# A hybrid layer on one core: 32x32 blocks in the triangular inverse, head sums in two fp32r passes, and another order on VectorE

## What is computed

```python
xn = rms_norm(h, norm_mix[l])
proj = xn @ w_l
y_a = chunk_band_attention(a_q, a_k, a_v, a_rel_bias[l])
y_b, v_l = rwkv7_time_mix(b_r, b_k, b_v, b_w, b_a, b_g, vmix, ...)
y_c = sliding_sink_attention(c_q, c_k, c_v, c_sinks[l], t5_bias)
h = h + concatenate([y_a, y_b, y_c]) @ w_out[l]
h = h + cross attention of rms_norm(h) into rms_norm(mem)
h = h + square(relu(rms_norm(h) @ mlp_w1[l])) @ mlp_w2[l]
return rms_norm(h, norm_final)

# in rwkv7_time_mix, per head of 64 features:
kk = kk / maximum(sqrt(sum(kk * kk)), 1e-12)           # a sum over a head's features
y = wkv7_scan(r, decay, k, v, -kk, kk * a)             # state = state*w + (state a) b + v k
var = mean(square(y - mean(y)))                        # a second one
bonus = sum(rh * kh * r_k) * vh                        # a third one
```

## Time and profile before

| what | us |
|---|---|
| median of three runs (2647.16 to 2648.95) | 2648.77 |
| the profiled execution | 2651.39 |
| its span | 2649.7 |
| TensorE busy | 2592.2 (98%) |
| VectorE busy | 1711.9 (65%) |
| ScalarE busy | 925.0 (35%) |
| GpSimd busy | 133.0 (5%) |

### The profile page before, as it was taken

The page is one execution under the profiler, slowest core; times in us unless marked ns, Lnnn a source line. Parts: engine busy times, 40 slices in busy tenths (PEclk is TensorE's granted clock), DMA queues, the critical chain, the costliest instruction groups (busy, mean ns, idle before and its releaser), DMA issues.

```text
span 2649.7 us, 45475 instructions
## 1 busy us (share of the span) xinstructions
PE 2592.2 (98%) x17994; PEld 2066.4 (78%) x17994; DVE 1711.9 (65%) x2535; ACT 925.0 (35%) x1475; POOL 133.0 (5%) x239
## 2 busy tenths in 40 slices
PE   9999999999999999998999999999999999999997
PEld 7877777777768765786878888888878888888886
DVE  6256666666634755344567677777777777777775
ACT  5222222222223644343533333333233332333324
POOL 5000101111112110000000000000000000000000
PEclk9999999999999999999999999999999999999999
DMA  4321111111125542221332332323323233232322
GB/s 168 119 62 51 50 45 50 49 50 50 49 90 202 180 133 66 88 88 48 111 105 88 112 105 95 114 87 110 111 90 113 88 110 109 91 119 87 105 88 104
DMA packets 72468, 250.13 MB, mean 94 GB/s; under 512 B 8960, under 2 KB 9088, under 8 KB 71104
## 3 DMA queue, kind: packets, MB, share of 16 engines
q1 hardware_dynamic: 65232, 222.62, 25.7%
q0 software_dynamic: 7024, 24.56, 2.9%
HBM read 236.93 MB, written 10.22 MB: 93 GB/s over the span
## 4 chain that ended last, share of the span: by engine, by line
PE 84%; DVE 8%; issue 4%; ACT 3%; DVEq 1%; DMA 0%; ACTq 0%; SPq 0%
PE ps L1435 25%; PE ps L1437 23%; PE ps L1436 23%; PE ps L1453 9%; DVE sum_lo L1334 2%; DVE b_raw L1279 1%; DVE w_lo L881 1%; DVE sums L1283 1%; PE ps L1662 1%; PE ps L1639 1%; DVE b_lo L1275 1%; ACT sums L807 1%; PE ps L1649 1%; PE ps L1447 1%; ACT b_hi L543 1%
## 5 line engine op out<-in xcount | busy, mean ns | idle before, releaser
L1435 PE MATMUL ps<-act_hi,w_hi 128*128 128x512 f32 x1792 | 730.4, 408 | 12.9 <-DVE w_lo L881 12.9
L881 DVE TENSOR_TENSOR w_lo<-w_raw,w_hi 128x1024 fp32r<-128x1024 f32 (+2 forms) x319 | 356.0, 1120 | 561.1 <-ACT w_hi L543 561.1
L1437 PE MATMUL ps<-act_hi,w_lo 128*128 128x512 f32 x1792 | 700.5, 391 | 0.0
L1436 PE MATMUL ps<-act_lo,w_hi 128*128 128x512 f32 x1792 | 700.3, 391 | 0.0
L543 ACT ACTIVATE w_hi<-w_raw 128x1024 fp32r<-128x1024 f32 (+2 forms) x319 | 310.3, 974 | 1014.6 <-PE ps L1437 1006.4
L1435 PEld LDWEIGHTS ps<-act_hi,w_hi 128*128 128x128 f32 x1792 | 336.4, 188 | 110.6 <-DVE w_lo L881 19.4
L1437 PEld LDWEIGHTS ps<-act_hi,w_lo 128*128 128x128 f32 x1792 | 336.9, 188 | 72.6
L1436 PEld LDWEIGHTS ps<-act_lo,w_hi 128*128 128x128 f32 x1792 | 337.1, 188 | 66.6 <-issue 4.3
L1435 PE MATMUL ps<-b_hi,sum_hi 128*128 128x512 f32 x848 | 330.5, 390 | 1.9 <-DVE sum_lo L1334 1.9
L1436 PE MATMUL ps<-b_lo,sum_hi 128*128 128x512 f32 x848 | 330.5, 390 | 0.0
L543 ACT ACTIVATE b_hi<-b_raw 128x1024 fp32r<-128x1024 f32 x210 | 221.1, 1060 | 302.1 <-PE ps L1437 300.4
(11 more groups left out here) (320 smaller groups left out, 2849.4 us busy)
## 6 DMA issues: line engine op xcount, KB each, us to landing
w_raw<-in_w_rest SPq DMA_DIRECT2D x200, 512.0 KB, 3.5
b_raw<-in_w_down SPq DMA_DIRECT2D x120, 512.0 KB, 3.4
w_raw<-in_w_pairs SPq DMA_DIRECT2D x112, 384.0 KB, 3.0
x_t<-in_x_turned SPq DMA_DIRECT2D x8, 512.0 KB, 8.1
qk<-scr_qkv POOLq DMA_DIRECT2D x16, 256.0 KB, 3.1
h<-in_x POOLq DMA_DIRECT2D x4, 1024.0 KB, 8.4
out<-h SPq DMA_DIRECT2D x4, 1024.0 KB, 3.9
scr_qkv<-pad POOLq DMA_DIRECT2D x15, 256.0 KB, 4.2
```

The costliest lines, as they stand in the source:

```text
L881: V.tensor_tensor(dst, w_raw[:, slot, 0:dst.shape[-1]], high.bitcast(F32), ALU.subtract).then_inc(s["w_split"], 1)
L1435: mm(dst, a_hi, b_hi, start=start, stop=False, skip_group_check=again)
L1436: mm(dst, a_hi, b_lo, start=False, stop=False, skip_group_check=again)
L1437: return mm(dst, a_lo, b_hi, start=False, stop=stop, skip_group_check=again)
```

## The change

It has four parts.

**The inverse by blocks.** LEVELS loses 32, so the levels build only the inverses of the four 32x32 diagonal blocks of a chunk (two heads x two halves). These are kept packed, four groups of 32 partitions by 8 chunks x 32 columns, 256 columns in all. The turned copy isn't kept: after each `level_t` TensorE turns `inv` (`inv_turned`), ScalarE copies it to `inv_b`, and `level_x` multiplies that by `t_level`. At the end `corner_t` and `corner_x` make the off-diagonal 32x32 corner. Each of these five is a loop of 32x32 matmuls, 32 in a call (16 for a corner). The gram for `m_ab` becomes `diagonal_grams`, 32 matmuls that read 64 rows each and write 32x32. T_PER_PAIR, X_PER_PAIR and V_PER_PAIR are the counts of semaphore steps in a pair.

**The head sums.** `ones2` and `mean2` are fp32r, and a sum is two fp32r matmuls, of the high and of the low part (`sums_of_split`). ScalarE therefore squares twice at p = 2 and p = 3 (the first one rounded to fp32r), VectorE forms the r*k product twice at p = 6, and VectorE has a new subtraction for each sum: at p = 3, at p = 4 (finishing pair), and at the end of p = 6. TensorE waits for these.

**The seam behind g = 14.** VectorE splits the first `rest` unit before the first of the three evacuations, ScalarE's high part waits for 119 used units, and the memory tokens' DMA is issued at the start of g = 13 and handled at positions 9 to 16.

**The feed-forward order.** On VectorE `up_lo(c, 2)` moves ahead of four of the `sum_low` calls and a weight sum, `up_lo(c, 3)` moves behind `op_lo` of product 3.

Tensors are also laid out anew in SBUF, and GpSimd's constants follow (fewer level masks, in more and smaller copies).

```diff
-LEVELS = [2, 4, 8, 16, 32]
+LEVELS = [2, 4, 8, 16]
...
+        def block_rows(k):
+            return slice(k * B, (k + 1) * B)
+
+        def block_cols(c, k):
+            return slice(c * L + k % 2 * B, c * L + (k % 2 + 1) * B)
+
+        def packed(c):
+            return slice(c * B, (c + 1) * B)
 
         def chunks(buf):
...
+                    nc.scalar.activation(sq_hi[:, :], kk_[:, :], ACT.Square, scale=col(prm, K_K))
...
+                    nc.scalar.activation(y2_hi[:, :], yc[:, :], ACT.Square)
...
+                if p in (14, 16, 18, 20) and elem:
+                    lv = (p - 14) // 2
+                    act.wait_ge(s["xT_mm"], V_PER_PAIR * q + lv + 1)
+                    copy(inv_b[:, :], ps[:, 5, NC * B:]).then_inc(s["xT_ev"], 1)
...
-            hi(0, UNITS * G_IN // RAW + 1, rest_slot(w_hi, 0), UNITS * G_IN)
+            hi(0, UNITS * G_IN // RAW + 1, rest_slot(w_hi, 0), UNITS * G_IN - 1)
...
+                    dve.wait_ge(s["sq_k"], q + 1)
+                    V.tensor_tensor(sq_lo[:, :], T1, sq_hi[:, :].bitcast(F32), ALU.subtract).then_inc(s["sq_split"], 1)
+                if p == 4 and fin:
+                    dve.wait_ge(s["ysq_ready"], f + 1)
+                    V.tensor_tensor(y2_lo[:, :], ysq[:, :], y2_hi[:, :].bitcast(F32),
+                                    ALU.subtract).then_inc(s["var_split"], 1)
...
-                    V.scalar_tensor_tensor(T1, rr[:, :], rk_col, kp[:, :], ALU.mult, ALU.mult).then_inc(s["bon_in"], 1)
+                    V.scalar_tensor_tensor(sq_hi[:, :], rr[:, :], rk_col, kp[:, :], ALU.mult, ALU.mult)
+                    V.scalar_tensor_tensor(T1, rr[:, :], rk_col, kp[:, :], ALU.mult, ALU.mult)
...
+                    V.tensor_tensor(sq_lo[:, :], T1, sq_hi[:, :].bitcast(F32), ALU.subtract).then_inc(s["bon_in"], 1)
...
-                    dve.wait_ge(s["mab_mm"], q + 1)
-                    masked(m_ab, 4, mk_lo[:, :])
...
+                    V.tensor_tensor(packed_chunks(inv[:, :]), packed_chunks(ps[:, 4, 0:NC * B]), over_chunks(mk_1[:, :]),
+                                    ALU.mult)
...
-                    dve.wait_ge(s["t_mm"], LV * q + lv + 1)
-                    masked(t_lev, 4, mk_lev[:, lv, :]).then_inc(s["t_ev"], 1)
+                    dve.wait_ge(s["t_mm"], T_PER_PAIR * q + lv + 1)
+                    if lv < len(LEVELS):
+                        V.tensor_tensor(packed_chunks(t_lev[:, :]), packed_chunks(ps[:, 4, 0:NC * B]),
+                                        over_chunks(mk_lev[:, lv, :]), ALU.mult).then_inc(s["t_ev"], 1)
+                    else:
+                        V.tensor_copy(t_lev[:, :], ps[:, 4, 0:NC * B]).then_inc(s["t_ev"], 1)
+                        dve.wait_ge(s["xT_mm"], V_PER_PAIR * q + lv + 1)
+                        masked(invT[par], 3, mk_upi[:, :]).then_inc(s["xT_ev"], 1)
...
+                    if lv < len(LEVELS):
+                        dve.wait_ge(s["x_mm"], X_PER_PAIR * q + lv + 1)
+                        V.tensor_tensor(inv[:, :], inv[:, :], ps[:, 5, 0:NC * B], ALU.add).then_inc(s["x_ev"], 1)
...
+                        if g == G_IN - 1 and u == UNITS - 1 and third == 0:
+                            lo(UNITS * G_IN, 0, rest_slot(w_lo, 0), rest_slot(w_hi, 0))
                         if g and u == UNITS - 1:
                             evacuate(g, third)
 
-            lo(UNITS * G_IN, 0, rest_slot(w_lo, 0), rest_slot(w_hi, 0))
...
                 sum_low(c - 1, A12, 2, 4)
+                up_lo(c, 2)
                 sum_low(c - 1, S2, 4, 4)
...
                         op_lo(c - 1, n + 2)
+                        if n == 1:
+                            up_lo(c, 3)
                         if n == 5:
...
+            def diagonal_grams(b, lhsT, rhs):
+                for c in range(NC):
+                    for k in (0, 2, 1, 3):
+                        hf, cols = HALF[k // 2], block_cols(c, k)
+                        last = mm(ps[block_rows(k), b, packed(c)], lhsT[hf, cols], rhs[hf, cols], start=True, stop=True)
...
+            def level_t(b):
+                for c in range(NC):
+                    for k in range(4):
+                        rows = block_rows(k)
+                        last = mm(ps[rows, b, packed(c)], m_abT[rows, block_cols(c, k)], inv[rows, packed(c)],
+                                  start=True, stop=True)
...
+            def level_x(b):
+                for c in range(NC):
+                    for k in range(4):
+                        rows = block_rows(k)
+                        last = mm(ps[rows, b, packed(c)], inv_b[rows, packed(c)], t_lev[rows, packed(c)],
+                                  start=True, stop=True)
...
+            def inv_turned(dst):
+                for c in range(NC):
+                    for k in range(4):
+                        rows = block_rows(k)
+                        last = mm(dst(c, k), inv[rows, packed(c)], eye_b[rows, :], start=True, stop=True)
...
+            def corner_t(b):
+                for c in range(NC):
+                    for k in (0, 2):
+                        last = mm(ps[block_rows(k + 1), b, packed(c)], m_abT[block_rows(k), block_cols(c, k + 1)],
+                                  inv[block_rows(k), packed(c)], start=True, stop=True)
...
+            def corner_x(b, whole):
+                for c in range(NC):
+                    for k in (0, 2):
+                        rows, cols = block_rows(k + 1), block_cols(c, k + 1)
+                        last = mm(ps[block_rows(k), b, cols], t_lev[rows, packed(c)], whole[rows, cols],
+                                  start=True, stop=True)
...
+            def sums_of_split(b, weights, high, low):
+                mm(bank(b), weights[:, :], high[:, :], start=True, stop=False)
+                return mm(bank(b), weights[:, :], low[:, :], start=False, stop=True)
...
                 if p == 4 and elem:
-                    pe.wait_ge(s["sq_k"], q + 1)
+                    pe.wait_ge(s["sq_split"], q + 1)
                     pe.wait_ge(s["zw_ev"], q + 1)
-                    mm(bank(4), ones2[:, :], T1, start=True, stop=True).then_inc(s["ss_mm"], 1)
+                    sums_of_split(4, ones2, sq_hi, sq_lo).then_inc(s["ss_mm"], 1)
...
-                    pe.wait_ge(s["ysq_ready"], f + 1)
+                    pe.wait_ge(s["var_split"], f + 1)
...
-                    mm(bank(3), mean2[:, :], ysq[:, :], start=True, stop=True).then_inc(s["var_mm"], 1)
...
+                    sums_of_split(3, mean2, y2_hi, y2_lo).then_inc(s["var_mm"], 1)
...
-                    mm(bank(5), ones2[:, :], T1, start=True, stop=True).then_inc(s["bon_mm"], 1)
+                    sums_of_split(5, ones2, sq_hi, sq_lo).then_inc(s["bon_mm"], 1)
...
-                    grams(4, aT[par], aa).then_inc(s["mab_mm"], 1)
+                    diagonal_grams(4, aT[par], aa)
...
                         grams(3, aa, rT[par]).then_inc(s["mrb_mm"], 1)
                         pe.wait_ge(s["inv_init"], q + 1)
                     else:
-                        pe.wait_ge(s["x_ev"], (LV - 1) * q + lv)
-                    grams(4, m_abT, inv).then_inc(s["t_mm"], 1)
+                        pe.wait_ge(s["x_ev"], X_PER_PAIR * q + lv)
+                    if lv < len(LEVELS):
+                        level_t(4).then_inc(s["t_mm"], 1)
+                        inv_turned(lambda c, k: ps[block_rows(k), 5, NC * B + c * B:NC * B + (c + 1) * B]
+                                   ).then_inc(s["xT_mm"], 1)
+                    else:
+                        corner_t(4).then_inc(s["t_mm"], 1)
+                        pe.wait_ge(s["mrb_ev"], q + 1)
+                        inv_turned(lambda c, k: ps[block_rows(k), 3, block_cols(c, k)]).then_inc(s["xT_mm"], 1)
...
-                    pe.wait_ge(s["t_ev"], LV * q + lv + 1)
-                    if lv:
-                        pe.wait_ge(s["xT_ev"], LV * q + lv)
-                    if lv < LV - 1:
-                        grams(5, invT[par], t_lev).then_inc(s["x_mm"], 1)
-                    pe.wait_ge(s["mrb_ev"], q + 1)
-                    grams(3, t_lev, invT[par]).then_inc(s["xT_mm"], 1)
+                    pe.wait_ge(s["t_ev"], T_PER_PAIR * q + lv + 1)
+                    pe.wait_ge(s["xT_ev"], V_PER_PAIR * q + lv + 1)
+                    if lv < len(LEVELS):
+                        level_x(5).then_inc(s["x_mm"], 1)
+                    else:
+                        corner_x(3, invT[par]).then_inc(s["xT_mm"], 1)
```

More of the change, by code:

```diff
@@ L103, in hybrid_layer @@
         sg, aa, cs = s2("sig_w", [P, SEQ]), s2("a_gate", [P, SEQ]), s2("cum_sig", [P, SEQ])
[L104 to L108, removed]
+        var_tmp = ExitStack()
+        s_var = alloc(var_tmp)
+        y2_hi, y2_lo = (s_var(n, [P, SEQ], F32R) for n in ("y_sq_hi", "y_sq_lo"))
+        var_tmp.close()
+        kkn, kk_dec = s2("kk_norm", [P, SEQ]), s2("k_dec", [P, SEQ])
+        g_inv, kp = s2("g_inv", [P, SEQ]), s2("k_mod", [P, SEQ])
+        m_abT = s2("m_abT", [P, SEQ])
```

(27 more changed lines are left out.)

95 lines of the change are left out of this document (46 added, 49 removed).

## The result

The change makes the kernel slower by a quarter of a per cent: 2654.56 us (median of 20 runs, 2647.19 to 2664.61) against 2648.67 before (2644.23 to 2651.62), ratio 1.0026 with a 95% interval of 1.0019 to 1.0033. I had forecast 2623 and a gain. The new kernel also scatters more than twice as widely, and its times go with the clock: its quickest execution had a mean granted clock of 0.994, its slowest one of 0.988. A mean lower by 0.006 over 2655 us is 16 of the 17 us between them.

A forecast was written before the change was run, and what follows sets the result against it. TensorE, busy throughout the pair groups, was taken as the bound. Inverse -29, sum passes -9.6, their waits +28, feed-forward -10.5, seam -4.5 took the profiled 2651.4 us to 2626, median 2623; range 2590 to 2670.

The forecast's parts named there:

- rival 3: Inverse: issue binds, 14.7 ns a small matmul, so blocks save nothing and shape changes cost extra; 2667 us, chance 0.12.
- How small records overlap: Inverse: four 32x32 matmuls run beside each other on four row groups, 32 ns a group, 0.51 us for 64.
- Rivals 2: Inverse: a small matmul costs about 11 ns however packed, 20 us worse in eight pairs; 2643 us, chance 0.14.
- 4: Inverse: every record takes its own 29 ns however few its columns, +124 us in place of -29; 2776, chance 0.10.
- Changes of shape: Inverse: 12 new changes between array shapes in a pair, 0.15 us each, cost 1.8 us a pair.
- the 8.7 us a pair: Inverse: cost of all small matmuls, replacing grams of 14.1 us; less 1.8 of shape changes, eight pairs gain 29 us.
- Masks and copies: Level positions: VectorE's smaller masks and ScalarE's four copies of 256 columns never make TensorE wait; costed at nothing.
- my three terms, 2.0 + 1.3 + 0.3: Head sums: new TensorE waits in us at p = 4, 8 and 10, taken as 3.5 a pair, 28 in eight.
- The gain of the passes, 9.6: Head sums: two fp32r passes take 0.46 us where one fp32 sum takes 0.85; 0.4 x 24 sums gained.
- a lower clock in the pair groups: Sign that the sum is wrong as a whole; the granted clock there was 1.00 before, and no cost was given.
- The feed-forward order: Feed-forward bodies: with `w_lo` moved earlier on VectorE, TensorE's 15 waits go, -10.5 us.
- The seam: Behind g = 14: splitting weights ahead of evacuations removes a 2.8 us wait and 1.7 us of low clock, -4.5 us.

The follow-up runs named there:

- fp32 sums: Kernel after with its three head sums as single fp32 matmuls again, without second squares, products and subtractions: 2628.41 us, ratio 0.9923.
- only the orders: Kernel before with only the two `up_lo` moved and the first `rest` unit split ahead of the evacuations: 2629.11 us, ratio 0.9925.
- the turns twice: Kernel after with single fp32 head sums and `inv_turned` issued twice in a row at positions 14, 16, 18 and 20: 2699.92 us, ratio 1.0192.

## Why the prediction was wrong

The forecast was 2623 and a gain with 0.71; it was a loss. That the time lies inside the range is luck: the range reached so far up for rival 3, whose mechanism is not what happened. By the steps:

- **How small records overlap: right.** Forecast 0.51 us for 64 records in fours, measured 0.54. Two starts 0.01 us apart were enough to tell four parts of the array from a floor for every record. Rivals 2 (0.70 us a call) and 4 are out. The sentence of the Trainium skill ("TensorE: Matmul & The Clock Gate", "Wait — 56ns, not 53.3ns?") that starts never come closer than about 25 ns does not hold across parts of the array: these come 8 ns apart on average. The bank rule that I cited from the Trainium skill ("TensorEngine Tiling (Array Packing)", "Gotcha 1: PSUM Pressure") does not bite here either: four row groups write one bank and go at once. `diagonal_grams` was even cheaper (0.68 us for 1.02).
- **Changes of shape: a little low.** The calls as measured are 8.6 us a pair (13 x 0.54, 0.68, and 0.9 for the two corners). The passages between main matmuls that no pause and no low clock touches add up to 3.4 us less a pair with fp32 sums than with only the orders. That leaves 14.1 - 8.6 - 3.4 = 2.1 us for a pair's twelve changes, 0.18 each where I took 0.15. So the array saved 27 us and not 29. Since these pair groups came out 0.4 us longer, 27 us and a bit were lost in them again: 5.1 to the clock and 22 to the pauses, 3 more than the list has, which counts them from a modelled end.
- **The step that failed: "A call ... is 64 records in 16 groups of four: 16 x 32 = 0.51 us", that is, a record costs array time alone.** From it came the 8.7 us a pair and the gain of 29. The sum has no term for the supply of instructions, nor for a lower clock. Masks and copies, which I did cost at nothing, held: no wait of TensorE on either stands in the list. I priced matmuls by the array and masks by their engines, and never asked where 7680 more instructions come from. Rival 3 had issue as the bound, but as a price of each record at a constant rate. Each record in fact runs at full speed, and then the engine stands still until a packet comes. So I looked for a limit in the spacing of neighbours, where there is none. The pauses and the clock behind them took back the blocks' whole gain. The rows could have warned: 147 packets against 17994 records stand on the page of the kernel before, and the level positions were going to hold 256 instructions and more in a microsecond. What they could not tell is how long a packet takes to be of use. The Trainium skill ("Runtime: NRT & Kernel Launch", "Instruction fetch mechanics") has the packets of 256 instructions, and says that crossing from one to the next is mostly hidden. In the kernel before that is so; in the kernel after it is 20.5 us.
- **The head sums: right in the main.** 26.9 us of waits against 28 (my three terms, 2.0 + 1.3 + 0.3, make 3.6 a pair and not 3.5). They are 14.8 at p = 4 and 12.1 at p = 8, forecast 16 and 10; the 0.3 for `a_dec` at p = 10 never came. The gain of the passes, 9.6, was not tried alone, but the sum for the pair groups closes with it. Not forecast: the stretches of low clock behind these waits. I had named a lower clock in the pair groups as a thing that would break the sum, and given it no price. Six stretches cost 10 us. With fp32 sums there are three, all behind pauses, so about half of the loss hangs on these waits and would not have come without them.
- **The feed-forward order: right mechanism, too small.** Forecast 10.5, measured 14.0. The list of waits counts idle time from the modelled end of the last matmul. From start to start the 15 waits are 12.8 us over the usual 0.23, and the first matmul behind each wait takes 0.11 longer, 1.7 more: 14.5.
- **The seam: right in what it removes.** The stretch behind the pair groups is 2.7 us shorter with only the orders (wait and clock gone, 1.6 of new wait on the evacuation) and 6.9 in the kernel after. The 4.2 between them come with one stretch of low clock less (6.8 us long, near 1242, which cost 3.4) and perhaps the memory tokens' move; that part I have not tried alone.

Added up for the profiled execution, in the pair groups: forecast -29 - 9.6 + 28 = -10.6, measured +25.8. The difference of 36 is 20.5 of pauses in the list and some 3 that it leaves out, 10 of clock, 2 of shape changes, -1 of waits, and some 2 that are not settled.

## What to carry to other kernels

When a change turns few large instructions into many small ones, count the instructions and ask how fast they come, not only how fast they run: on TensorE here 256 instructions every 3.3 us, with a stock of some 300 that a run of large matmuls leaves full. The signs are waits on "issue" inside a loop without semaphores, and a page whose instruction packets have grown. The cure was to spread them, and better, to give part of them to an engine that does the same work in one instruction. A wait of TensorE can have a second price, 1.7 us for each 3.4 us at half clock behind it: four of the eight waits at p = 4 here had it, and none of the seven of 1.3 us for `state`. It belongs into the sum as a chance, not as nothing.

## What the runs showed of the hardware

- Four 32x32 matmuls in different row groups start some 8 ns apart on average (64 records in 0.54 us), also with one PSUM bank for all.
- In the pair groups an instruction packet of 16 KB lands 0.9 to 1.7 us after its start, and a TensorE that ran dry goes on 2.2 to 2.9 us after that start. Two packets are never under 3.2 us apart.
- Every pause of instruction supply, 32 in the kernel after and 51 with the turns twice, falls at the same place of a block of 256 instructions. A packet starts at most some 300 instructions ahead of the place where TensorE would run dry.
- The scatter of the kernel after, 2647 to 2665 us, goes with its mean granted clock, 0.994 to 0.988. The kernel with fp32 sums has nearly the same pauses and lies between 2627.6 and 2629.3 in five executions. So the pauses alone do not make it.
- VectorE's transposition of eight 32x32 fp32 blocks on each of four groups of 32 partitions takes 0.45 us, as much as an addition of the same size (0.42).
